# Attention: the sums are turned back one query tile later, and each group's value products run in two parts

## The reference

```python
def banded_attention(q, k, v, past, slopes, dist_scale, sinks=None):
    ...
    s = jnp.einsum('nbqgrd,nbkgd->ngrbqk', qb, kb) * (hd ** -0.5)
    s = jnp.where(mask, s + bias, -jnp.inf)
    m = jnp.max(s, axis=-1)
    ...
    p = jnp.exp(s - m[..., None])
    den = jnp.sum(p, axis=-1)
    ...
    o = jnp.einsum('ngrbqk,nbkgd->nbqgrd', p, vb)
    o = (o / den.transpose(0, 3, 4, 1, 2)[..., None]).reshape(n, L, G, R, hd)

def reference(...):
    h = rmsnorm(x, g_mix_pre[l])
    z = h @ w_in[l]
    o_a = nsa_mixer(...)       # compressed, chosen (top-8 blocks of 64) and window attention, gated
    o_b = dilated_mixer(...)   # three dilations (1, 4, 16) x 4 heads, merged by their log-sums
    o_c, _ = banded_attention(cq, ck, cv, WIN_C - 1, sl_c, 1, sinks=sinks[l])
    mix = jnp.concatenate([o_a, o_b, o_c], axis=-1) @ w_out[l]
    x = x + rmsnorm(mix, g_mix_post[l])
    f = conv_glu_ffn(rmsnorm(x, g_ffn_pre[l]), w_up[l], conv_w[l], conv_b[l], w_down[l])
    x = x + rmsnorm(f, g_ffn_post[l])
```

## Time and profile before

| | us |
|---|---|
| median of 3 runs | 3414.16 |
| lowest and highest | 3414.13, 3419.08 |
| the profiled execution, its own time | 3413.19 |
| its span | 3411.4 |
| PE busy in the span | 3272.4 (96%) |
| DVE, ACT, POOL busy | 1412.3, 1193.2, 602.1 |
| granted clock, mean | 0.993 |

### The profile page before, as it was taken

The page is one execution under the profiler, slowest core; times in us unless marked ns, Lnnn a source line. Parts: engine busy times, 40 slices in busy tenths (PEclk is TensorE's granted clock), DMA queues, the critical chain, the costliest instruction groups (busy, mean ns, idle before and its releaser), DMA issues. The chain is left out here.

```text
span 3411.4 us, 46500 instructions
## 1 busy us (share of the span) xinstructions
PE 3272.4 (96%) x16834; PEld 2652.8 (78%) x16834; DVE 1412.3 (41%) x3866; ACT 1193.2 (35%) x2459; POOL 602.1 (18%) x551
## 2 busy tenths in 40 slices
PE   8999999998998899999989999999999999999998
PEld 6888888887776666666668878887888888888887
DVE  5111101105767887777755444304440344115421
ACT  5111111115666765655543333203330233013310
POOL 1566653530000013332110000000000000000000
PEclk9999999999999999999999999999999999999999
DMA  5789976657878733442247865656556655665553
GB/s 190 268 314 324 327 256 210 222 182 186 207 185 207 180 86 76 101 101 57 78 115 229 257 251 193 240 184 247 194 189 246 235 193 190 246 237 196 197 193 140
DMA packets 299259, 676.10 MB, mean 198 GB/s; under 512 B 99392, under 2 KB 154944, under 8 KB 284864
## 3 DMA queue, kind: packets, MB, share of 16 engines
q1 hardware_dynamic: 265344, 517.80, 47.9%
q0 software_dynamic: 33696, 155.40, 12.6%
HBM read 495.93 MB, written 185.57 MB: 200 GB/s over the span
## 5 line engine op out<-in xcount | busy, mean ns | idle before, releaser
L543 PE MATMUL z_banks<-h_hi,z_w_hi 128*128 128x512 f32 x972 | 381.2, 392 | 0.0
L543 PE MATMUL z_banks<-h_hi,z_w_lo 128*128 128x512 f32 x972 | 378.4, 389 | 0.0
L1640 PE MATMUL banks<-low,f_own 128*128 128x512 f32 x1344 | 313.5, 392 | 11.5 <-DMA f_own<-f_lo 6.1
L1424 ACT ACTIVATE w_small<-w_small,a_stats 128x128 f32<-128x128 f32 (+3 forms) x510 | 257.4, 517 | 143.9 <-DVE a_stats L1510 98.9
L1640 PEld LDWEIGHTS banks<-low,f_own 128*128 128x128 f32 x1344 | 254.5, 190 | 66.4 <-issue 13.2
L1354 PE MATMUL a_ot_ps<-a_turned_w,vs 128*64 128x256 f32 (+3 forms) x1452 | 223.4, 431 | 0.0
L1321 PE MATMUL a_t_ps<-idt,w_small 128*128 128x128 f32 x1092 | 219.2, 280 | 0.8 <-DVE a_turned_w L1413 0.8
L323 ACT ACTIVATE st_hi<-z_banks 128x512 fp32r<-128x512 f32 (+1 forms) x100 | 59.8, 598 | 442.7 <-PE z_banks L543 318.0
L1510 DVE CUSTOM_DVE_ANT_0 w_small<-a_s_ps,near 128x128 f32<-128x128 f32 (+2 forms) x456 | 165.4, 392 | 113.9 <-PE a_s_ps L1310 86.2
L543 PEld LDWEIGHTS z_banks<-h_hi,z_w_hi 128*128 128x128 f32 x972 | 182.7, 188 | 36.9
L461 DVE TENSOR_TENSOR st_lo<-z_banks,st_hi 128x512 fp32r<-128x512 f32 x76 | 52.3, 692 | 384.1 <-ACT st_hi L323 307.8
(11 more groups left out here) (263 smaller groups left out, 7071.4 us busy)
## 6 DMA issues: line engine op xcount, KB each, us to landing
f_own<-f_hi SPq DMA_DIRECT2D x88, 512.0 KB, 3.7
f_own<-f_lo SPq DMA_DIRECT2D x88, 512.0 KB, 4.6
z_xs<-in_w_ffn POOLq DMA_DIRECT2D x33, 1024.0 KB, 8.3
f_hi<-z_v_hi POOLq DMA_DIRECT2D x33, 1024.0 KB, 5.1
f_lo<-z_xs POOLq DMA_DIRECT2D x33, 1024.0 KB, 5.8
low<-z_hi SPq DMA_DIRECT2D x48, 512.0 KB, 8.0
k_hi<-f_hi SPq DMA_DIRECT2D x44, 512.0 KB, 3.7
k_hi<-f_lo SPq DMA_DIRECT2D x44, 512.0 KB, 4.6
```

The costliest lines, as they stand in the source:

```text
L543: last = pe.matmul(banks[:, 4 * k + n, :], w[:, k, c, :], h[c][:, tok], start=(c == order[0] and q == 0), stop=(c == DC - 1 and q == 2))
L1424: act.activation(weights(n), weights(n), ACT.Exp, bias=negm[:, n % 32:n % 32 + 1], scale=-1.0, accum_out=total).then_inc(weighed, 1)
L1640: last = pe.matmul(out, w[:, c * P:(c + 1) * P], rows[:, c, :], start=(c == 0 and x == 0), stop=(c == DC - 1 and x == 2))
```

## The change

Two things are moved in `attend`, and nothing is computed otherwise.

- `values_in`: the products of group g come in two runs, the first half of the list (rounded up) at the end of step 4g+5, the rest at the end of step 4g+6. The single product of a k unit falls into the first run, so it is one step earlier.
- `turn_out` on PE, `finish` on DVE and `add_rows` on POOL come in step 4g+10, one later. All loops run one step longer. `take_out` on ACT stays at step 4g+8.

```diff
--- before.py
+++ after.py
@@ -951,7 +951,8 @@
         g, third = divmod(n - 5, 4)
         if third == 3 or not 0 <= g < N // 4:
             return g, 0, 0
-        return g, 0, len(value_steps(g)) if third == 1 else 0
+        count = len(value_steps(g))
+        return g, (0, (count + 1) // 2, 0)[third], ((count + 1) // 2, count, 0)[third]
 
     pick_batch = {batch["pick"]: b for b, batch in enumerate(batches) if "pick" in batch}
     steps = {"b": 1, "c": 3, "w": 2, "s": 2, "k": 5}
@@ -1248,7 +1249,7 @@
                 pool.wait_ge(upper_added, g - late + 1)
                 pool.tensor_tensor(rows, rows, add[:, :, HD:2 * HD], ALU.add).then_inc(out_done, 1)
 
-            for n in range(first_chosen * NT, N + 6):
+            for n in range(first_chosen * NT, N + 7):
                 if n - 2 in mix_steps:
                     t = mix_steps.index(n - 2)
                     mix_pairs(t)
@@ -1261,8 +1262,8 @@
                     pool.wait_ge(ob_done, t + 1)
                     pool.dma_start(o_mid[t * P:(t + 1) * P, :], o_b[:, t % 2].rearrange("p h d -> p (h d)"))\
                         .then_inc(ob_out[t % 2], 16)
-                if n % 4 == 1 and (n - 9) // 4 >= late:
-                    add_rows((n - 9) // 4)
+                if n % 4 == 2 and (n - 10) // 4 >= late:
+                    add_rows((n - 10) // 4)
             for k in range(2):
                 pool.wait_ge(ob_out[k], 16 * (NT // 2))
 
@@ -1376,7 +1377,7 @@
                     last = pe.transpose(t_ps[0:NS, b % TB, i, :], unsel[:, 4 * q + i, :], idt[:])
                 last.then_inc(turned, 1)
 
-            for n in range(N + 6):
+            for n in range(N + 7):
                 g, start, end = values_in(n)
                 some = chunks(n) if n < N else [(None, 0, 0)]
                 for x, (piece, a, z) in enumerate(some):
@@ -1384,8 +1385,8 @@
                         scores(*piece)
                     if z > a:
                         turn(n, a, z)
-                    if x == 0 and n >= 9 and (n - 9) % 4 == 0:
-                        turn_out((n - 9) // 4)
+                    if x == 0 and n >= 10 and (n - 10) % 4 == 0:
+                        turn_out((n - 10) // 4)
                     if x == len(some) - 1 and end > start:
                         weigh_values(g, start, end)
                 if n in chosen_at:
@@ -1619,8 +1620,8 @@
                     take(dve, 1, [b for b in closing[n] if batches[b]["u"] is None])
                 if n == 7:
                     gates_and_sinks()
-                if n >= 9 and (n - 9) % 4 == 0:
-                    finish((n - 9) // 4)
+                if n >= 10 and (n - 10) % 4 == 0:
+                    finish((n - 10) // 4)
 
 
 AHEAD = 4
```

## The result

| | before | after |
|---|---|---|
| median, us | 3414.16 | 3500.29 |
| lowest and highest, us | 3411.01, 3420.13 (5 runs) | 3497.31, 3506.51 (5 runs) |
| ratio | | 1.0248, 95% interval 1.0234 to 1.0262 |
| span of the profiled execution, us | 3411.4 | 3496.1 |

The changed kernel is 86 us slower. I had said slower, 3463 us, range 3420 to 3490: the sign is right, the size is 37 us short and outside the range.

The account below looks back on a forecast made before the run. PE was taken to bound the kernel, by its own work and its waits. More runs +40, uneven halves +43, copy waits -22, waits before turns and scores -12: +49 us, so 3463 us, range 3420 to 3490.

Parts of the forecast that it names:

- The price of a run and of uneven halves: On PE, 120 more value runs at 0.33 us add 40 us; 25,856 more columns at 1.67 ns add 43 us.
- That wait goes: In 17 of 24 sliding groups and some others, PE's wait for ACT's copy vanishes: -22 of 51 us.
- DVE's finish keeps `on_ps` longer, but the next turning back is a group away: On DVE, finish one step later holds its buffer longer, but the next turning back is 3 to 7 us away.
- For k the product comes a step earlier behind the same wait: 0: In compressed (k) units, moving the single product one step earlier costs 0 us.
- Waits in front of turns in the chosen and window heads, -12: Two runs with work between level waits for turns and scores: half of 24 us saved, between 0 and -24.
- No load is late: SP's store waits one step longer, but its next wait ends several steps after that; any cost is under 1 us.
- all waits stay: Rival 1: added work delays everybody, turning back behind the first run makes DVE's finish late; +83 - 8, 3488 us, chance 0.15.
- Rival 2: All waits go, since two short runs give DVE and ACT scores sooner: +83 - 51 - 24 = +8, 3422 us, chance 0.15.
- Rival 3: A run's price is hidden by weights loaded early during turns: +43 - 51 - 12 = -20, 3394 us, chance 0.05.
- idle in front of L1368: Sign in the changed profile: PE's idle in front of this line would be nearly nil.
- The sign for telling the rivals apart: PE's wait before L1355 for ACT's `a_ot`, with tails: near 25 us forecast, near 45 rival 1, under 8 rival 2.
- The two signs of being wrong: Second runs start without the 0.2 us gap, or both array halves work at once across the cut.

Follow-up runs that it names:

- the later runs: Changed kernel with both value runs of a group one step later (ends of 4g+6 and 4g+7), turning back still at 4g+10: 3420.8 us.
- the split alone: Changed kernel with turning back, finish and additions back at 4g+9, the two value runs kept at 4g+5 and 4g+6: 3457.0 us.
- the later turning back alone: Changed kernel with all value products in one run at the end of 4g+6, turning back, finish and additions kept at 4g+10: 3395.6 us.

## Why the prediction was right in sign and short by 37 us

- **The price of a run and of uneven halves: about right.** The second run of a sliding group lasts from 1214.81 to 1215.61, 0.80 us (0.81 worked out), and starts 0.20 us after the turn in front of it. A column of the longer half costs 1.63 to 1.69 ns in three kinds (1.67). For the run by itself, four sliding units in a row: 15.26 us each in two even runs a group, with no wait listed; 14.82 in one run, with one wait of 0.42 and its tail of 0.16. That is (15.26 - 14.24) / 4 = 0.26 us a run (0.33 worked out; over 120 runs 8 us less). The k units say where it comes from. Their product takes 97 columns of the array instead of 64, and it starts 0.12 us after the turn in front of it (1027.85 to 1027.97) and lasts 0.86 us for 512 columns, 1.67 ns each with nothing added. Five products of 64 need 1.02 for the same 512. So both the 0.17 and the later start go with the products on half of the array. By the Trainium skill ("TensorEngine Tiling (Array Packing)", "Key Properties") a change of tiling mode drains the engine. These rows fit that, but no run here tells a drain from something else.
- **"That wait goes", -22 us: the step that failed.** I followed one semaphore, ACT's copy, and saw that it would come in time. But the turning back was put behind the first run, and that run waits for takes as well. 40.7 us in front of the turning back became 45.5 us in front of the run. My check that "DVE's finish keeps `on_ps` longer, but the next turning back is a group away" asked who waits for the finish's buffer, not what stands behind the finish in DVE's own list: a take that the next first run waits for. The sliding heads grew by 19.4 us instead of some 10: a group takes 5.1 us (20.4 a unit), of which over four units 11.3 us in 16 waits, with tails 0.87 each, are waits in front of the first run. The 4.2 that remain are PE's own work, for which I had 4.42; with the later runs and no listed wait a group takes 4.34. DVE's waits for the turning back, which I had expected to shrink, doubled from 47.8 to 94.9 us.
- **"For k the product comes a step earlier behind the same wait: 0": failed too, and the larger miss.** The wait is the same, but what is queued behind it is the turning back, and behind that finish, take and biases. The k units took 15 us more. Giving them their old places back won 27 in all, and moving PE's turning back alone in front of their product took them from 108.5 to 85.1 us. With the sliding heads' excess of 9 to 10 the 27 make up the 37 us, though that is in part a coincidence: up to 8 of the 27 may be the clock's, and in the other kinds misses of both signs cancel (fold 16 +10.5 us instead of some 5, with 10 us of the lower clock in one of its units; window and chosen heads together +12.5 as forecast).
- **Waits in front of turns in the chosen and window heads, -12: about right.** 15.0 us became 6.6, and 6.3 in front of wide scores 4.3. With the split alone they are 4.5 and 2.7. (The 24 us with tails that the 12 is half of should have been nearer 26: 20.8 us and 0.16 for each of 31 waits.)
- **"No load is late": wrong, by little.** The load of the first chosen head's mask came late, 3.5 us in the changed kernel (it landed at 1306.72, the scores started at 1306.92) and 7.9 where the rest was faster.
- **Of the rivals** the first, "all waits stay", was nearest: 3488 us, by the very mechanism (the turning back behind the first run makes DVE's finish late). I gave it 0.15 since I took the finish's new place behind two biases for a gain. It too left out that the waits can grow. Rival 2's end, with hardly a wait for the copy left, exists, but needs the later runs: 2.3 us there, and 3420.8 us against the 3422 that I had worked out for the changed kernel; that the two are so near is chance. Rival 3 fell with the price of a run.
- **Of the signs I had named,** idle in front of L1368 is nearly nil as said. The sign for telling the rivals apart was badly chosen. It named the waits in front of L1355 for ACT's `a_ot`: these are 14.5 us, with tails 18, nearest to the 25 of my forecast. All waits in front of L1355 are 45.5 us, with tails 56, and of these 45.5 the profile puts two thirds down to something else than the copy. PEld's idle in front of the loads of L1355 grew, as said, from 77.6 us in 332 times to 130.1 in 398. A sliding group takes 5.1 us, not 4.4. The two signs of being wrong didn't show: second runs start with the gap of 0.20, and the halves don't work at once across the cut. The failure came from a place for which I had no sign.

What stays open: why a finish at 4g+11 hurts the window and chosen heads, and how the 36 us between the split alone (3457.0) and the same split with everything one step later (3420.8) divide. The waits for ACT's copy, 31.6 us in 50 and 2.3 in 4, with tails differ by 36.7 us, which would be all of it. But they don't say which of the moved steps takes them away; a kernel with the later runs and with turning back and finish at 4g+9 would, and there is none. Open is also what the lower clock of the first stage costs; the bounds given here take every part of it as time on the path.

## What to carry to other kernels

When an instruction is moved, don't ask only whether its own semaphore will be there (in this case `a_ot_taken`). List everything that the instructions now in front of it wait for: an in-order queue gives it all their waits. What feeds another engine's chain (here four transposes of 0.4 us) belongs in front of bulk work that itself waits for that engine. And when work is cut in two on an array whose halves run side by side, cut each half's list evenly.

## What the runs showed of the hardware

A store of 512 KB and the reload that waits for it took 4.2 us before the change and 7.9 in the later turning back alone, where loads issued in front of it were landing for 5.9 us of it instead of 1.1.

Products of 64 columns on half of the array, between transposes on all of it, start 0.20 us after a transpose and take 0.16 to 0.17 us beyond 1.67 ns a column of the longer half, with two products in a run (0.59 us for 256 columns, in the even halves) as with sixteen. The product of 97 columns starts 0.12 us after and takes 1.67 ns a column. Halves that are filled one after the other instead of side by side cost the sum: 1.63 to 1.69 ns in three kinds of heads, and 1.48 in the sliding heads, for each column by which the longer halves grew.

Moving the value runs (0.9 to 6.6 us each) by one step, with no work added, moved the whole kernel by 116 us.
